# Forgetting attention: rows of gate sums and of norms padded with zeros from 48 to all 128 partitions in the products that use them

## The reference, cut to what matters

```
proj = h @ w_in
q, k, v, z, f_logit = split(proj)                 # 16 heads of 128
q = rms_norm(q, q_norm_g); k = rms_norm(k, k_norm_g)
log_f = log_sigmoid(f_logit + f_bias)
c = cumsum(log_f, axis=1).transpose(0, 2, 1)      # one row of gate sums for each head
logits = q @ k^T * scale + c[t] - c[s]            # causal
o = softmax(logits) @ v
x = x + (o * silu(z)) @ w_out
```

## Time and profile before

| what | value |
|---|---|
| median of 3 runs | 1614.92 us (1612.04 to 1615.39) |
| the profiled execution's own time | 1615.93 us |
| its span, first to last instruction | 1614.1 us |
| PE busy, PEld busy | 1575.9 us (98%), 1431.5 us (89%) |
| DVE, ACT, POOL busy | 1013.3 us (63%), 825.8 us (51%), 504.5 us (31%) |
| mean granted TensorE clock | 0.989 of full speed |

### The profile page before, as it was taken

One profiled execution on the slowest core, in us unless ns is written; L12 is line 12 of the kernel. 1 busy time (PEld: TensorE's weight loads), 2 busy tenths in 40 slices (PEclk: granted clock), 3 DMA queues, 4 the chain that ended last, 5 costly groups with the idle time before them and its releaser, 6 DMA issues.

```text
span 1614.1 us, 27456 instructions
## 1 busy us (share of the span) xinstructions
PE 1575.9 (98%) x10572; PEld 1431.5 (89%) x10572; DVE 1013.3 (63%) x2102; ACT 825.8 (51%) x1527; POOL 504.5 (31%) x470
## 2 busy tenths in 40 slices
PE   7999999999999999999999999999999999999998
PEld 6888899887889999999888889988877778999998
DVE  5899867354666686665399997644244445675532
ACT  3676656434555544444266666444245445454442
POOL 1777534332222200000067764255111122000043
PEclk9999999999999999999999999999999999999999
DMA  6554455464633578775254536555541112666653
GB/s 187 143 159 134 131 185 179 159 140 123 128 107 132 157 192 209 197 195 185 82 156 136 152 118 199 138 157 163 151 131 53 53 40 92 205 173 186 176 163 116
DMA packets 327333, 237.43 MB, mean 147 GB/s; under 512 B 18049, under 2 KB 314371, under 8 KB 327204
## 3 DMA queue, kind: packets, MB, share of 16 engines
q1 hardware_dynamic: 315736, 228.70, 48.7%
q10 hardware_dynamic: 11468, 6.98, 2.1%
HBM read 233.93 MB, written 1.74 MB: 146 GB/s over the span
## 4 chain that ended last, share of the span: by engine, by line
PE 83%; DVE 9%; ACT 5%; issue 2%; DMA 1%; POOL 1%; DVEq 0%; SPq 0%; ACTq 0%; POOLq 0%
PE bank L733 17%; PE bank L735 7%; PE bank L736 7%; PE bank L737 7%; PE bank L1167 4%; PE bank L1484 3%; PE bank L784 3%; PE bank L786 3%; PE bank L785 3%; PE bank L1485 3%; PE bank L1486 3%; DVE bank L1040 2%; PE bank L747 2%; DVE wlo L377 2%; ACT whi L368 1%
## 5 line engine op out<-in xcount | busy, mean ns | idle before, releaser
L377 POOL TENSOR_TENSOR wlo<-ring,whi 128x1024 fp32r<-128x1024 f32 (+3 forms) x112 | 256.8, 2297 | 695.0 <-ACT whi L368 695.0
L368 ACT CAST whi<-ring 128x1024 fp32r<-128x1024 f32 (+3 forms) x352 | 340.2, 985 | 244.0 <-PE bank L737 83.0
L377 DVE TENSOR_TENSOR wlo<-ring,whi 128x1024 fp32r<-128x1024 f32 (+4 forms) x240 | 310.5, 1302 | 234.8 <-ACT whi L368 233.2
L733 PE MATMUL bank<-sqb,ring 128*128 128x256 f32 x1536 | 341.1, 382 | 5.1 <-DVE sqb L631 5.1
L733 PEld LDWEIGHTS bank<-sqb,ring 128*128 128x128 f32 x1536 | 294.2, 192 | 47.5 <-issue 5.7
L983 POOL TENSOR_TENSOR scratch<-scratch 128x256 f32<-128x256 f32 x288 | 200.4, 733 | 362.6 <-ACT scratch L929 353.2
L735 PE MATMUL bank<-xh,whi 128*128 128x256 f32 x928 | 265.4, 286 | 0.3 <-DVE xl L653 0.3
L736 PE MATMUL bank<-xl,whi 128*128 128x256 f32 x928 | 263.8, 284 | 0.0
L737 PE MATMUL bank<-xh,wlo 128*128 128x256 f32 x928 | 263.7, 284 | 0.0
L1040 DVE SCALAR_TENSOR_TENSOR bank<-scratch,convw,bank 128x256 f32<-128x256 f32 x576 | 231.1, 482 | 0.0
L735 PEld LDWEIGHTS bank<-xh,whi 128*128 128x128 f32 x928 | 179.3, 193 | 5.8 <-issue 5.3
(11 more groups left out here) (300 smaller groups left out, 2948.6 us busy)
## 6 DMA issues: line engine op xcount, KB each, us to landing
ring<-in_a_w_in_dram SPq DMA_DIRECT2D x64, 512.0 KB, 5.2
ring<-in_b_w_in_dram SPq DMA_DIRECT2D x32, 1024.0 KB, 5.9
ring<-in_c_w_in_dram SPq DMA_DIRECT2D x64, 512.0 KB, 5.4
ring<-in_w_in_dram SPq DMA_DIRECT2D x26, 1024.0 KB, 5.2
ring<-in_w_ffn_in_dram SPq DMA_DIRECT2D x44, 512.0 KB, 5.0
ring<-in_a_w_in_dram SPq DMA_DIRECT2D x16, 1024.0 KB, 5.1
ring<-in_a_w_out_dram SPq DMA_DIRECT2D x16, 1024.0 KB, 5.3
ring<-in_w_ffn_out_dram SPq DMA_DIRECT2D x16, 704.0 KB, 4.5
```

Source lines behind the costliest of these rows:

```text
L368: nc.scalar.copy(piece(whi, h)[:, :, 0:n], src).then_inc(hi_done, 1)
L377: engine.tensor_tensor(piece(wlo, h)[:, :, 0:n], src, piece(whi, h)[:, :, 0:n].bitcast(F32), ALU.subtract).then_inc(done, 1)
L733: mm = nc.tensor.matmul(o, halves[h][1][:, k, :], sqb[:, k, :], start=(k == 0), stop=(k == KD - 1))
```

## The change

The tables take all 128 partitions instead of 48; rows 48 to 127 are cleared with the rest and stay zero, as do their entries in `c_sel` (there the identity matrix has zeros). The products that read them contract over 128 partitions. The low parts still go to partitions 32 to 47. The list of instructions on every engine and their order are unchanged; only shapes differ: the 80 products with tables (64 in L1167, 16 in L1545) and five DVE instructions (L1396 to L1399 and L1435) go from 48 to 128 partitions. In the changed file the lines behind L1267 stand one lower.

```diff
-        c_rows = 32 + FH
+        c_rows = P
+        f_low = slice(32, 32 + FH)
         c_sel = y_lo[0:c_rows, 16, 0:FH]
         c_hl, c_neg = y_lo[0:c_rows, 17, :], y_lo[0:c_rows, 18, :]
         rr_hl = [y_lo[0:c_rows, 19:21, :].rearrange("p a t -> p (a t)"), std_r[0:c_rows, :]]
...
-                nc.vector.tensor_tensor(rr_hl[stage][32:c_rows, :], rr[0:FH, :], rr_hl[stage][0:FH, :].bitcast(F32), ALU.subtract)\
+                nc.vector.tensor_tensor(rr_hl[stage][f_low, :], rr[0:FH, :], rr_hl[stage][0:FH, :].bitcast(F32), ALU.subtract)\
                     .then_inc(f_lo, 1)
...
-                        nc.vector.tensor_tensor(c_hl[32:c_rows, :], csum, c_hl[0:FH, :].bitcast(F32), ALU.subtract).then_inc(f_c, 1)
+                        nc.vector.tensor_tensor(c_hl[f_low, :], csum, c_hl[0:FH, :].bitcast(F32), ALU.subtract).then_inc(f_c, 1)
```

## The result

The changed kernel took 1600.83 us (median of 4 runs, 1598.92 to 1604.11) against 1615.13 us for the kernel before (4 runs). The ratio is 0.9918 with a 95% interval of 0.9898 to 0.9938: 14.3 us less, and by the interval between 10.0 and 16.5. Its profiled execution took 1600.63 us with a span of 1598.8 us; the span before was 1614.1.

What follows compares the result with a forecast made beforehand. PE was taken to bound the attention loop, losing time at each change of partition number. Savings of 11.4 (heads), 3.0 (single spreads) and 0.95 (pairs) sum to 15.4 us: 1599.5 us, range 1596.3 to 1603.7.

Steps and rivals of the forecast that it cites:

- single spreads: Eight spreads standing alone in slots of the attention loop: two partition changes each, 0.38 us saved each, 3.0 us in all.
- Heads: Eight q x k and table products in each of 16 heads: 1.83 us shrinks to 1.12, saving 11.4 us in all.
- Pairs: The other eight spreads, run as four pairs: 0.95 us saved, the last pair's second spread waiting for DVE's scaling.
- Feeders: Rival: in eight loop iterations DVE's logits, delayed by ACT's bank eviction, hold up PE; 1602.7 us, chance 0.06.
- Format: Rival: switches between fp32 and fp32r cause the gaps, so 48 of the heads' 64 stay; 1608.0 us, chance 0.04.
- Step-0 operand: Rival: the table products' reading of one repeated column holds back the load, so nothing changes; 1614.9 us, chance 0.02.
- Slower: Rival: loads are drawn ahead only if row groups differ, so 124 gaps replace 88; 1621.4 us, chance 0.03.

Runs made afterwards that it cites:

- one of two: Changed kernel, but the first of the two table products of each half head contracts over 48 partitions again: 1612.50 us, ratio 0.9978.
- grouped order: Kernel before, 48 partitions kept, but in each head both q x k products come first, then the four table products: 1608.87 us, ratio 0.9958.
- heads-only kernel: Changed kernel, but the spreads contract over 48 partitions again; only the heads' table products take 128: 1604.52 us, ratio 0.9929.
- order on 128: Changed kernel, all on 128 partitions, with both q x k products of a head before its four table products: 1601.43 us, ratio 0.9904.

## Why the prediction was right

*Where the time was lost.* The 0.2 us behind each change of partition number was read as PE standing still inside its queue. After the change the loads of the loop's table products and single spreads start with the matmul ahead of them, with the same instructions in the same order, and two experiments that move the changes move the gaps with them (one of two; grouped order). That PE runs empty in a gap is read from the late starts; the traces don't show the inside of the array.

*What causes it.* The prediction named the number of partitions, from two rows. That was right for the change made and too wide as a rule. "Each time the number of partitions changes" fails at 65 and 96: a product over 65 or 96 partitions beside one over 128 has no gap, one over 64 has. For 48 turned into 128 both rules give the same time, so the forecast could not suffer from it. The gap belongs to the border between at most 64 and more. The page "TensorEngine Tiling (Array Packing)" of the Trainium skill, section "Key Properties", has the words for it: "Changing tiling mode (not just tile) drains the TensorE"; its section "Available Configurations" lists halves of 64 rows as a configuration of their own. The runs fit that: the load behind a crossing starts 0.20 us late, and a change costs 0.16 to 0.21 us. They don't show the mode of a product, so the name for the cause is the page's and not measured.

*What both kernels still pay.* Nor is an equal number of contracted rows enough. The sums of squares for the norms (L1481, L1480 before) contract over 128 partitions like the projections ahead of them, but their weights are 16 columns wide. In the changed kernel:

```profile
283.05 0.28 PE L1487 MATMUL bank<-xh,wlo 128*128 128x256 f32 x1
283.26 0.11 PEld L1481 LDWEIGHTS bank<-scratch,cst 128*16 128x16 f32 x2
```

The load comes 0.20 to 0.21 us behind the matmul, at each of the four places in this stage and in both kernels, with no releaser named. So narrow weights seem to have a gap of the same size; no experiment varied their width.

*Heads.* Predicted 0.71 us a head, 11.4 in all. Measured 1.83 less 1.11 = 0.72; over the loop 129.72 - 115.96 = 13.76, and 0.72 more for head 15, is 14.5 us, against 11.4 + 3.0 = 14.4 predicted for heads and single spreads.

*Single spreads.* Predicted 0.38 us each; the heads-only kernel puts them at 0.40 to 0.43, 3.3 us for eight instead of 3.0. Head 0's new wait on ACT took about 0.3 us of the loop's gain back. The prediction had looked for such a wait at the low halves of the weights, and it came at the bank eviction.

*Pairs.* Predicted 0.95 us instead of 1.52, since the last pair's second spread waits for DVE. From the matmul before the first pair to head 0 it was 379.67 - 342.51 = 37.16 us and is 379.36 - 343.17 = 36.19: 0.97 less. The wait grew to 0.60 us, inside the 0.6 to 0.8 stated.

*Feeders.* DVE keeps up. Its instructions for the logits (L1178) now wait for PE 6 times for 4.4 us around the loop, where it was 10 times for 11.2; PE waits for no `wlo` there.

*The sum.* 14.5 + 0.97 = 15.4 us by the traces' own parts, 15.4 predicted, and the span fell by 15.3. That agreement is better than the traces allow: the changed kernel's execution came to the stage 0.66 us later (343.17 against 342.51), before any change, and won about as much elsewhere. The medians differ by 14.3 us, inside their interval.

*The rivals.* Format: out (the changed kernel itself, one of two, the order on 128). Step-0 operand: out, since the table products still read it and their loads are drawn ahead. Slower: out; the padded products use the same rows as all others, and their loads start with the matmul before (379.48). The Trainium skill's rule in "TensorE: Matmul & The Clock Gate", by which loads overlap only where the row group differs, stands in its section "The mechanism" and not in the one that the prediction names. It doesn't hold for these loads; the same section also lets a load run ahead when it goes to the background weight buffer, which would fit them, and no run here shows where a load goes.

*Slips.* The prediction said that the table products would stand under L1168; the line lies ahead of the inserted one and is still L1167. The format rival's sum, 16 x 0.18 + 3.0 + 0.95, is 6.8 and not 6.9 us.

## What to carry to other kernels

Look at the starts of weight loads, not at busy time: a load that comes 0.2 us after the matmul before it, with no semaphore behind it, is a load that was not drawn ahead. Where products over at most 64 partitions stand between products over 128, either make their contraction longer than 64 with rows of zeros (here a load took 190 ns instead of 184, hidden behind the matmul before), or put them side by side so that fewer changes are left. It pays as far as TensorE sets the pace in that stretch; where another engine does, PE's wait for it grows by what was won, as the 0.43 us that became 0.83.

## What the runs showed of the hardware

In these kernels a contraction over 65 or 96 partitions behaves in a stream of 128-partition products like one over 128 (load 190 ns, drawn ahead); over 48 or 64 it does not (load 0.18 us, held back), and a crossing costs 0.16 to 0.21 us at full clock, as a mean over entering and leaving. The table products themselves are not longer for more partitions: with their loads drawn ahead, a head's eight products take 1.11 us with 96 and 65 as with 128. A product over 128 partitions with weights of 16 columns also has its load 0.21 us late. Whether entering and leaving cost the same wasn't measured apart.
